# A transformer block pair with product-key experts: 48 instead of 32 tokens by gathered expert rows, the dense part over 208 instead of 224 tokens

## The chip, the cores and the metric

One core of a Trainium2 chip runs the kernel. The metric is the device time of one execution in microseconds; the kernel before has a median of 3184.81 over three runs (3183.85 to 3185.70).

## The reference

256 tokens of width 2048 go through a first block (mixer with a state-space half and an attention half, then an expert layer) and a second one (attention and convolution, cross attention to a memory, a feed-forward part of width 8192). The change is in the expert layer, `peer`: of 16384 experts each token takes 8 x 16, with weights g, by the best sums of two sets of 128 keys.

```
def block(args):
    tb, ib, gb = args
    act = jax.nn.gelu(jnp.einsum('thkd,td->thk', u[ib], tb), approximate=False)
    return jnp.einsum('thk,thkd->td', gb * act, v[ib])
```

u[ib] and v[ib] are rows of two 16384 x 2048 matrices. All is float32.

## The kernel before, in words

**The weight stream.** All weights come as 532 units of 128 x 2048 float32 (1 MB), loaded by SyncE into a ring of four buffers `raw`. Each matmul is done in split precision: ScalarE writes the high part of a unit (`w_hi`, rounded to fp32r; `ahead_first` casts three quarters of it and `ahead_rest` the rest), VectorE writes the low part (`w_lo` = raw - w_hi, line 1033, called `ahead`), and TensorE adds hi x hi, hi x lo and lo x hi. `w_hi` and `w_lo` have two buffers each, so the split of unit u + 2 starts when unit u's matmuls are over, and must be done before unit u + 1's are. The order of the work on each engine is written out by hand, unit by unit; the engines wait for each other by semaphores.

**Dense experts.** Of the 256 tokens the last 224 (`TD`) are computed densely, against all experts, in eight rounds of 2048 experts: 16 u units (`u0` to `u7`: hidden values of 128 experts each) and 16 e units (`e0` to `e7`: 128 output columns each). A matrix of gate values, zero for experts that a token did not pick, is built in u1 (groups of four tokens: one-hot products `pick_a`, `pick_b` on VectorE, lines 1424 and 1429, a matmul, an eviction, blocks of 16 tokens written to DRAM) and read back per round by GpSimd (`load_gates`). In u0 and u1 a unit is 48 single matmuls of 224 columns (`feature_unit`). From e0 on it is a paired unit (`paired_unit`, lines 1768, 1769 and 1774): 16 times one matmul of 448 columns (w_hi against both parts of the activations) and one of 224 (w_lo against the high part).

In rounds 2 to 7 a u unit goes like this: ScalarE copies one half of the sum out of PSUM (line 876), VectorE adds the other (`pair_add`, 1493), ScalarE applies gelu (880), and `gating` on VectorE multiplies by the gates (1447), casts to the high part (1506) and subtracts for the low part (1507). In an e unit `accumulate` adds two halves to `accT` (1486, 1487). At unit 15 of a u half VectorE does the split for the second e unit after the gating, at the others before it.

**Gathered experts.** The first 32 tokens (`G`) are computed from gathered rows. 128 partitions are 4 x 32: partition p holds token p mod 32 and a quarter of its 128 picks. So 32 gathers of 128 rows of u, and 32 of v (GpSimd, line 567, into two buffers `got`), serve all picks. Each gather feeds one *job* on VectorE over 128 x 2048: for u a product with a row sum (1517, with `h_rows`, the normalised tokens), for v a multiply and add into `acc_rows` (1522). The jobs are set between the units by a table: in a round, units 1, 4, 7, 10, 13 of the u half and 0, 2, ... 14 of the e half, 13 jobs. In u7 `sel_rows` adds the four parts with 32 small matmuls (2081), and `sel_add` copies the result to `accT`. In u7 also the memory input is loaded, squared and normalised; in e7 its tiles are turned (`turn_tile`), one per unit.

Of the kernel before, what the change touches and what calls it, by code (L numbers as in the profile page):

```python
# [15 lines left out]
F32 = mybir.dt.float32  # L16
# [21 lines left out]
G = 32  # L38
GROUPS_G, GJ = P // G, PICKS // (P // G)
# [87 lines left out]
def build(nc, x_in, mem_in, stream, cols_in, consts_in, rows_in, wide_in, wdtf_in, keys_in,  # L127
          rel_in, onehot_in, u_rows, v_rows, out):
    ctx = ExitStack()
    with ctx:  # L130
# [47 lines left out]
        row_rs = sb("row_rs", [P, 1])  # L178
# [83 lines left out]
        h_rows = at("h_rows", [P, D], F32, pk)  # L262
        acc_rows = at("acc_rows", [P, D], F32, pk)
# [84 lines left out]
        rows_done = sem("rows_done")  # L348
        s_got = [sem(f"s_got{i}") for i in range(2)]
# [78 lines left out]
        JOBS_U, JOBS_E = (1, 4, 7, 10, 13), tuple(range(0, 16, 2))  # L428
        JOB_AT, _n = {}, 0
        for _r in range(2, PEER_ROUNDS - 1):  # L430
            for _kind, _ks in (("u", JOBS_U), ("e", JOBS_E)):
                for _k in _ks:
                    if _n < 2 * GJ:
                        JOB_AT[_kind, _r, _k] = _n
                        _n += 1
        assert _n == 2 * GJ
        ROW_ACT_AT = next(at for at, n in JOB_AT.items() if n == GJ)
# [68 lines left out]
        def _(pool):  # L506
# [47 lines left out]
            for c in range(GROUPS_G):  # L554
                ps, js = slice(c * G, c * G + G), slice(c * GJ, c * GJ + GJ)
                eng.dma_start(row_idx[ps, :], pick_idx[:, js]).then_inc(s_idx, 16)
                eng.dma_start(row_gate[ps, :], picked[0:G, 0, 2, js]).then_inc(s_idx, 16)
                eng.dma_start(row_rs[ps, :], stat[0:G, 2:3]).then_inc(s_idx, 16)
# [12 lines left out]
            for i in range(2):  # L571
                eng.wait_ge(g_write[i], 16 * (TBLOCKS // 2))
# [6 lines left out]
            eng.wait_ge(s_idx, 16 * 3 * GROUPS_G)  # L579
# [4 lines left out]
            for c in range(GROUPS_G):  # L584
                eng.dma_start(h_rows[c * G:c * G + G, :], x_d[0:G, :]).then_inc(s_rows, 16)
            eng.wait_ge(rows_done, 1)
# [15 lines left out]
            eng.dma_start(wide_l[:, :], wide_in[0:1, :].partition_broadcast(P)).then_inc(s_wide, 16)  # L602
            eng.wait_ge(g_used, 16 * PEER_ROUNDS)
            eng.dma_start(xm[:, :, :], x_d.rearrange("(t p) d -> p t d", p=P)).then_inc(s_xm, 16)
            eng.wait_ge(pow_set, 1)
# [19 lines left out]
        def _(act):  # L625
# [56 lines left out]
            def square(name, src, tt):  # L682

                junk = junk_early if name in ("ln1", "ln2") else junk_cross if name == "gcross" else \
                    acc_rows if name == "gmem" else junk_late
# [183 lines left out]

            for r in range(2, PEER_ROUNDS):  # L870
                for k in range(16):
# [8 lines left out]
                    eng.activation(tmp[:, j, 0:TD], tmp[:, j, 0:TD], ACT.Gelu).then_inc(tmp_full, 1)  # L880
                    if k == 15:
                        ahead_rest(u)
                    if ("u", r, k) == ROW_ACT_AT:
                        eng.wait_ge(got_used, GJ)
                        eng.activation(row_dot[:, :], row_dot[:, :], ACT.Gelu, scale=row_rs[:, :]).then_inc(row_act, 1)
                    if r == PEER_ROUNDS - 1 and k in (6, 8):
                        eng.wait_ge(sel_done, 1)
                        eng.wait_ge(s_mem, 16)
                        square("gmem", mem, (k - 6) // 2)
                if r == PEER_ROUNDS - 1:  # L890
                    break
                for k in range(16):
                    ahead_first(UNIT0[f"e{r}"] + k)
                    ahead_rest(UNIT0[f"e{r}"] + k)
                    if ("e", r, k) == ROW_ACT_AT:
                        eng.wait_ge(got_used, GJ)
                        eng.activation(row_dot[:, :], row_dot[:, :], ACT.Gelu, scale=row_rs[:, :]).then_inc(row_act, 1)
# [8 lines left out]
            for j in range(16):  # L906
                if j == 0:
                    scaled_tile("gmem", 0)
                if j < 15:
                    scaled_tile("gmem", j + 1)  # L910
# [6 lines left out]

# [108 lines left out]
        def _(dve):  # L1026
# [422 lines left out]
            def gated0(g):  # L1449
# [5 lines left out]
                if g % 2 == 0:  # L1455
                    eng.wait_ge(g_write[g // 2], 16 * (TBLOCKS // 2))
# [8 lines left out]
            def gated1(k):  # L1465

                if k == 0:
                    eng.wait_ge(s_idx, 16 * 3 * GROUPS_G)
# [885 lines left out]
```

## Time and profile before

| | before |
|---|---|
| median of 3 runs | 3184.81 us |
| the profiled execution | 3187.75 us |
| its span | 3185.9 us |
| granted TensorE clock, mean | 0.989 |
| TensorE busy | 3067.4 us (96%), 19428 matmuls |
| VectorE busy | 2237.3 us (70%) |
| ScalarE busy | 1400.6 us (44%) |
| data moved | 673 MB, 211 GB/s |

The span runs from the first to the last instruction of the program; the execution's own time is 1.85 us longer. The shares are over the whole span. The dense experts take up the stretch from about 562 to 1946 us: u0, u1, e0 and e1 to 970, then six rounds of a u and an e half. Matmuls overlap each other in the records, so their pace is read from the distance of their starts and not from their durations.

### The profile page before, as it was taken

Reading aid. Unit: us, or ns where it says so; the run is one execution under the profiler, and the core shown is the slowest. Engines: PE = TensorE matmul, PEld = TensorE weight load, DVE = VectorE, ACT = ScalarE, POOL = GpSimd, SP = SyncE. Lnnn points to the kernel's source line nnn. Section 1 sums busy time; section 2 is a strip of 40 time slices with the busy share of each in tenths; the row PEclk is TensorE's granted clock in tenths of the full one; section 3 lists DMA queues with packets and bytes.
Section 4 is the critical chain, followed back from the end, with each engine's and each line's share of the span. In section 5 each row is a group of like instructions: output and inputs, shape, how many; then the busy total and the mean of one; then the engine's idle time right before and its main releaser. Section 6 shows DMA issues by size and latency. Waiting matters only on the chain.

```text
span 3185.9 us, 49641 instructions
## 1 busy us (share of the span) xinstructions
PE 3067.4 (96%) x19428; PEld 2810.2 (88%) x19428; DVE 2237.3 (70%) x3255; ACT 1400.6 (44%) x1640; POOL 143.3 (4%) x168
## 2 busy tenths in 40 slices
PE   6999989999999999999999999999898999999997
PEld 6898879899999999999999999998787888888886
DVE  4666548999867888888888677687655646555564
ACT  3465443356444444444444445334444333333332
POOL 1000000000101101010101000000000000000000
PEclk9999999999999999999999999999999999999999
DMA  4433454456767888888888664544343555555553
GB/s 186 178 141 131 146 197 148 170 189 235 244 245 279 314 300 311 298 310 300 308 298 312 239 238 172 186 166 152 130 174 107 197 190 189 188 188 194 186 188 126
DMA packets 95548, 673.14 MB, mean 211 GB/s; under 512 B 11528, under 2 KB 11552, under 8 KB 15424
## 3 DMA queue, kind: packets, MB, share of 16 engines
q1 hardware_dynamic: 77184, 562.07, 48.9%
q0 software_dynamic: 16224, 94.72, 8.8%
q10 hardware_dynamic: 2016, 14.68, 1.2%
q8 instruction: 80, 1.31, 0.2%
q14 instruction: 44, 0.36, 0.0%
HBM read 652.48 MB, written 18.89 MB: 211 GB/s over the span
## 4 chain that ended last, share of the span: by engine, by line
PE 85%; DVE 11%; ACT 2%; issue 1%; DMA 0%; DVEq 0%; SPq 0%; POOL 0%; POOLq 0%; ACTq 0%
PE bank L1768 29%; PE bank L1769 15%; PE bank L1796 6%; PE bank L1798 6%; PE bank L1797 6%; PE bank L1746 6%; PE bank L1748 5%; PE bank L1747 5%; DVE w_lo L1033 4%; PE bank L1774 2%; DVE pick_a L1429 1%; ACT w_hi L631 1%; DVE pick_b L1424 1%; PE bank L1860 1%; PE bank L1824 1%
## 5 line engine op out<-in xcount | busy, mean ns | idle before, releaser
L1033 DVE TENSOR_TENSOR w_lo<-raw,w_hi 128x2048 fp32r<-128x2048 f32 x532 | 1218.3, 2290 | 570.1 <-ACT w_hi L631 548.1
L1768 PE MATMUL bank<-a_both,w_hi 128*128 128x448 f32 (+1 forms) x3840 | 1258.3, 380 | 6.9 <-DVE a_both L1050 3.9
L1769 PE MATMUL bank<-a_both,w_lo 128*128 128x224 f32 (+1 forms) x4096 | 1060.5, 269 | 0.0
L1768 PEld LDWEIGHTS bank<-a_both,w_hi 128*128 128x128 f32 x3840 | 721.4, 188 | 90.3 <-DVE a_both L1050 4.4
L1769 PEld LDWEIGHTS bank<-a_both,w_lo 128*128 128x128 f32 x4096 | 778.2, 190 | 11.6
L631 ACT ACTIVATE w_hi<-raw 128x2048 fp32r<-128x2048 f32 x308 | 588.4, 1911 | 409.3 <-PE bank L1798 399.7
L1746 PE MATMUL bank<-a_both,w_hi 128*128 128x256 f32 (+1 forms) x1984 | 571.2, 288 | 19.3 <-DVE w_lo L1033 14.0
L644 ACT ACTIVATE w_hi<-raw 128x1536 fp32r<-128x1536 f32 x224 | 333.6, 1489 | 570.2 <-PE bank L1769 568.8
L1747 PE MATMUL bank<-a_both,w_hi 128*128 128x256 f32 (+1 forms) x1984 | 559.2, 282 | 0.0
L1748 PE MATMUL bank<-a_both,w_lo 128*128 128x256 f32 (+1 forms) x1984 | 559.1, 282 | 0.0
L1746 PEld LDWEIGHTS bank<-a_both,w_hi 128*128 128x128 f32 x1984 | 383.4, 193 | 26.9 <-issue 12.5
L1747 PEld LDWEIGHTS bank<-a_both,w_hi 128*128 128x128 f32 x1984 | 383.5, 193 | 0.3
L1748 PEld LDWEIGHTS bank<-a_both,w_lo 128*128 128x128 f32 x1984 | 383.1, 193 | 0.0
L1796 PE MATMUL bank<-w_hi,a_both 128*128 128x512 f32 x960 | 378.6, 394 | 4.3 <-DVE a_both L1677 3.4
L1798 PE MATMUL bank<-w_hi,a_both 128*128 128x512 f32 x960 | 375.8, 392 | 0.0
L1797 PE MATMUL bank<-w_lo,a_both 128*128 128x512 f32 x960 | 375.7, 391 | 0.0
L1796 PEld LDWEIGHTS bank<-w_hi,a_both 128*128 128x128 f32 x960 | 181.8, 189 | 43.1 <-issue 5.0
L1798 PEld LDWEIGHTS bank<-w_hi,a_both 128*128 128x128 f32 x960 | 181.5, 189 | 38.5
L1797 PEld LDWEIGHTS bank<-w_lo,a_both 128*128 128x128 f32 x960 | 181.6, 189 | 37.4
L1768 PE MATMUL bank<-e_both,w_hi 128*128 128x448 f32 x480 | 152.3, 374 | 0.0
L650 ACT ACTIVATE w_hi<-raw 128x512 fp32r<-128x512 f32 x224 | 138.3, 617 | 0.0
L1769 PE MATMUL bank<-e_both,w_lo 128*128 128x224 f32 x512 | 130.3, 265 | 0.0
(314 smaller groups left out, 2436.8 us busy)
## 6 DMA issues: line engine op xcount, KB each, us to landing
raw<-stream_dram SPq DMA_DIRECT2D x532, 1024.0 KB
gates_scratch<-stage ACTq DMA_DIRECT2D x14, 1024.0 KB, 4.8
gbuf<-gates_scratch POOLq DMA_DIRECT2D x30, 448.0 KB, 6.9
x<-x_dram SPq DMA_DIRECT2D x2, 1024.0 KB, 6.5
x_scratch<-x POOLq DMA_DIRECT2D x1, 2048.0 KB, 11.0
wide<-wide_dram POOLq DMA_DIRECT2D x2, 1024.0 KB, 9.0
mem<-mem_dram POOLq DMA_DIRECT2D x1, 2048.0 KB, 9.6
xm<-x_scratch POOLq DMA_DIRECT2D x1, 2048.0 KB, 9.0
```

Source lines behind the costliest of these rows:

```text
L631: eng.activation(w_hi[k % SPLIT][:, :], raw[:, k % RAW, :], ACT.Copy).then_inc(hi_done, 1)
L644: eng.activation(w_hi[k % SPLIT][:, 0:PART], raw[:, k % RAW, 0:PART], ACT.Copy)
L650: eng.activation(w_hi[k % SPLIT][:, PART:UNIT], raw[:, k % RAW, PART:UNIT], ACT.Copy).then_inc(hi_done, 1)
L1033: eng.tensor_tensor(w_lo[k % SPLIT][:, :], raw[:, k % RAW, :], w_hi[k % SPLIT][:, :].bitcast(F32), ALU.subtract).then_inc(split_done, 1)
L1746: mm(o, hi[:, ks], tile(0, kt), start=kt == 0, stop=False)
L1747: mm(o, hi[:, ks], tile(1, kt), start=False, stop=False)
L1748: last = mm(o, lo[:, ks], tile(0, kt), start=False, stop=kt == KT - 1)
L1768: mm(o, hi[:, ks], pair, start=kt == 0, stop=False)
L1769: inst = mm(o2, lo[:, ks], pair[:, 0, :], start=False, stop=False, skip_group_check=True)
L1796: mm(o, tile(0, k0 + k)[:, ts], hi[:, ns], start=first and k == 0, stop=False)
L1797: mm(o, tile(0, k0 + k)[:, ts], lo[:, ns], start=False, stop=False)
L1798: last = mm(o, tile(1, k0 + k)[:, ts], hi[:, ns], start=False, stop=end and k == 3)
```

## The change

- 48 tokens instead of 32 are computed by gathered rows, in two sets: tokens 0 to 31 with four parts of picks, tokens 32 to 47 with eight parts of 16 picks. There are 48 + 48 gathers and jobs instead of 32 + 32, and two tiles `set_rows` in the place of `h_rows` and `acc_rows`.
- The dense part has 208 columns: matmuls of 416 and 208 in the paired units, 208 in u0 and u1, 13 blocks and 52 groups of gate values instead of 14 and 56.
- The table of jobs has 8 in a u half and 10 in an e half, up to u7's unit 11.
- The cast of the activations' high part goes from VectorE to ScalarE, one unit behind: in unit k ScalarE casts that of unit k - 1 after its gelu, and VectorE subtracts for k - 1 after the multiplication by the gates for k. At unit 15 both do 14 and 15.
- `sel_rows` runs once per set (u7 units 3 and 4, e7 units 0 and 1). Squares, normalisation and turns of the memory input move into e7, with two tiles a unit from unit 5 to 9.

```
-G = 32
-GROUPS_G, GJ = P // G, PICKS // (P // G)
+SETS = [(0, 32), (32, 16)]
+G = GJ = sum(n for _, n in SETS)
+SET_DMAS = sum(P // n for _, n in SETS)
...
-        JOBS_U, JOBS_E = (1, 4, 7, 10, 13), tuple(range(0, 16, 2))
+        JOBS = {"u": (1, 3, 5, 7, 9, 11, 13, 14), "e": (0, 2, 3, 5, 6, 8, 9, 11, 13, 15)}
+        JOBS_LAST = (1, 3, 5, 7, 9, 11)
...
+        GMEM_AT = {5 + j: (2 * j, 2 * j + 1) for j in range(5)}
+        GMEM_AT.update({10 + j: (10 + j,) for j in range(6)})
...
-            for c in range(GROUPS_G):
-                eng.dma_start(h_rows[c * G:c * G + G, :], x_d[0:G, :]).then_inc(s_rows, 16)
-            eng.wait_ge(rows_done, 1)
+            for i, (t0, n) in enumerate(SETS):
+                for c in range(P // n):
+                    eng.dma_start(set_rows[i][c * n:c * n + n, :], x_d[t0:t0 + n, :]).then_inc(s_rows, 16)
+            eng.wait_ge(rows_done, len(SETS))
...
+            def cast(r, k):
+
+                eng.wait_ge(g_used, 16 * r + k + 1)
+                eng.activation(a2[0][:, k, 0:TD], tmp[:, k % 4, 0:TD], ACT.Copy).then_inc(act_hi, 1)
...
                     eng.activation(tmp[:, j, 0:TD], tmp[:, j, 0:TD], ACT.Gelu).then_inc(tmp_full, 1)
+                    if k >= 1:
+                        cast(r, k - 1)
                     if k == 15:
                         ahead_rest(u)
+                        cast(r, 15)
...
-                own.do(eng.tensor_copy(a2[0][:, k, 0:TD], t))
-                eng.tensor_tensor(a2[1][:, k, 0:TD], t, a2[0][:, k, 0:TD].bitcast(F32), ALU.subtract).then_inc(tmp_split, 1)
+            def act_lo(r, k):
+
+                eng.wait_ge(act_hi, 16 * (r - 2) + k + 1)
+                eng.tensor_tensor(a2[1][:, k, 0:TD], tmp[:, k % 4, 0:TD], a2[0][:, k, 0:TD].bitcast(F32), ALU.subtract)\
+                    .then_inc(tmp_split, 1)
...
-                    gating(r, k)
+                    gate_hidden(r, k)
+                    if k > 0:
+                        act_lo(r, k - 1)
                     if k == 15:
+                        act_lo(r, 15)
                         ahead(UNIT0[f"u{r}"] + k)
...
-                        eng.tensor_tensor(h_rows[:, :], h_rows[:, :], wide2[:, :], ALU.mult).then_inc(rows_done, 1)
+                        for i in range(len(SETS)):
+                            eng.tensor_tensor(set_rows[i][:, :], set_rows[i][:, :], wide2[:, :], ALU.mult).then_inc(rows_done, 1)
...
-                if k in (2, 3):
-                    sel_rows(k - 2)
+                if k in (3, 4):
+                    sel_rows(0, k - 3)
...
+                if j in (0, 1):
+                    sel_rows(1, j)
+                if j == 5:
+                    eng.wait_ge(sel_added, 2)
                     eng.wait_ge(normed, 6)
```

What stands in a row on the engines at two places (a row is line, operation, output<-inputs, shape; w_lo is the split, `tmp<-tmp,bank` the sum of the halves, `tmp<-tmp,gbuf` the multiplication by the gates, `got,row_dot` or its second row a job).

VectorE, units 14 and 15 of the u half of round 3 and the first e unit, before:

```order
L1493 TENSOR_TENSOR tmp<-tmp,bank 128x224
L1033 TENSOR_TENSOR w_lo_52<-raw,w_hi_50 128x2048
L1447 TENSOR_TENSOR tmp<-tmp,gbuf 128x224
L1506 CAST a_both<-tmp 128x224
L1507 TENSOR_TENSOR a_both<-tmp,a_both 128x224
L1493 TENSOR_TENSOR tmp<-tmp,bank 128x224
L1447 TENSOR_TENSOR tmp<-tmp,gbuf 128x224
L1506 CAST a_both<-tmp 128x224
L1507 TENSOR_TENSOR a_both<-tmp,a_both 128x224
L1033 TENSOR_TENSOR w_lo_53<-raw,w_hi_51 128x2048
L1486 TENSOR_TENSOR accT<-bank,accT 128x224
```

and with the change:

```order
L1517 TENSOR_TENSOR tmp<-tmp,bank 128x208
L1057 TENSOR_TENSOR w_lo_52<-raw,w_hi_50 128x2048
L1471 TENSOR_TENSOR tmp<-tmp,gbuf 128x208
L1532 TENSOR_TENSOR a_both<-tmp,a_both 128x208
L1545 ISA got,row_dot<-got,set_rows_139 128x2048
L1545 ISA row_dot 128x1
L1517 TENSOR_TENSOR tmp<-tmp,bank 128x208
L1471 TENSOR_TENSOR tmp<-tmp,gbuf 128x208
L1532 TENSOR_TENSOR a_both<-tmp,a_both 128x208 x2
L1057 TENSOR_TENSOR w_lo_53<-raw,w_hi_51 128x2048
L1510 TENSOR_TENSOR accT<-bank,accT 128x208
```

The casts are gone, a job stands between units 14 and 15, and the two subtractions for 14 and 15 stand together ahead of the split.

ScalarE at unit 15 of the same half, before:

```order
L644 ACTIVATE w_hi_51<-raw 128x1536
L876 ACTIVATE tmp<-bank 128x224
L880 ACTIVATE tmp<-tmp 128x224
L650 ACTIVATE w_hi_51<-raw 128x512
L644 ACTIVATE w_hi_50<-raw 128x1536
```

and with the change:

```order
L658 ACTIVATE w_hi_51<-raw 128x1536
L900 ACTIVATE tmp<-bank 128x208
L904 ACTIVATE tmp<-tmp 128x208
L892 ACTIVATE a_both<-tmp 128x208
L664 ACTIVATE w_hi_51<-raw 128x512
```

The cast for unit 14 follows the gelu, and the one for unit 15 comes after the rest of the weight cast (a further L892 row).

## Rows read from the trace of the kernel before

**Rows 1.** The page, part 4: the chain that ended last, shares by engine.
```profile
PE 85%; DVE 11%; ACT 2%; issue 1%; DMA 0%; DVEq 0%; SPq 0%; POOL 0%; POOLq 0%; ACTq 0%
```

**Rows 2.** Stretches u3 and e3: length, busy us per engine, PEclk, DMA share, GB/s.
```profile
1133.00:1214.00 81.00, 81.00 (x518) 77.15 (x517) 69.03 (x87) 40.57 (x61) 8.13 (x8) 1.00 0.83 294
1214.00:1293.00 79.00, 79.00 (x505) 75.17 (x504) 64.28 (x69) 32.51 (x34) 8.65 (x9) 1.00 0.86 315
```

**Rows 3.** Timeline of DVE: start, us; splits at the ends of e3 and up1.
```profile
1214.49 2.29 DVE L1033 TENSOR_TENSOR w_lo<-raw,w_hi 128x2048 fp32r<-128x2048 f32 x1
...
1375.27 2.29 DVE L1033 TENSOR_TENSOR w_lo<-raw,w_hi 128x2048 fp32r<-128x2048 f32 x1
...
2634.05 2.29 DVE L1033 TENSOR_TENSOR w_lo<-raw,w_hi 128x2048 fp32r<-128x2048 f32 x1 [3.23 <-ACT w_hi L631]
...
2724.69 2.29 DVE L1033 TENSOR_TENSOR w_lo<-raw,w_hi 128x2048 fp32r<-128x2048 f32 x1
```

**Rows 4.** Timeline of PE: matmuls in u0, the selection in u7, a pair in u4.
```profile
595.87 0.27 PE L1747 MATMUL bank<-a_both,w_hi 128*128 128x224 f32 x1
...
597.54 0.27 PE L1747 MATMUL bank<-a_both,w_hi 128*128 128x224 f32 x1
...
1790.13 1.84 PE L2081 MATMUL bank<-consts,acc_rows 128*128 128x32 f32 x15
...
1340.01 0.26 PE L1769 MATMUL bank<-a_both,w_lo 128*128 128x224 f32 x1
1340.11 0.37 PE L1768 MATMUL bank<-a_both,w_hi 128*128 128x448 f32 x1
```

**Rows 5.** Groups of DVE instructions, whole span: busy, mean ns | idle before.
```profile
L1033 DVE TENSOR_TENSOR w_lo<-raw,w_hi 128x2048 fp32r<-128x2048 f32 x532 | 1218.3, 2290 | 570.1 <-ACT w_hi L631 548.1 <-ACT w_hi L650 8.2
...
L1517 DVE CUSTOM_DVE_ANT_0 got<-got,h_rows 128x2048 f32<-128x2048 f32 x32 | 73.1, 2283 | 0.0
L1522 DVE SCALAR_TENSOR_TENSOR acc_rows<-got,row_gate,acc_rows 128x2048 f32<-128x2048 f32 x31 | 72.7, 2345 | 0.0
...
L1506 DVE CAST a_both<-tmp 128x224 fp32r<-128x224 f32 x96 | 26.6, 277 | 3.3
```

**Rows 6.** Timeline of DVE at the end of u3.
```profile
1213.96 0.38 DVE L1493 TENSOR_TENSOR tmp<-tmp,bank 128x224 f32<-128x224 f32 x1
...
1219.91 2.28 DVE L1033 TENSOR_TENSOR w_lo<-raw,w_hi 128x2048 fp32r<-128x2048 f32 x1
1222.54 0.39 DVE L1486 TENSOR_TENSOR accT<-bank,accT 128x224 f32<-128x224 f32 x1 [0.35 <-PE bank L1774]
```

**Rows 7.** Groups of ACT instructions from 1054 to 1776 us.
```profile
L644 ACT ACTIVATE w_hi<-raw 128x1536 fp32r<-128x1536 f32 x144 | 214.5, 1490 | 373.4 <-PE bank L1769 373.4
L650 ACT ACTIVATE w_hi<-raw 128x512 fp32r<-128x512 f32 x144 | 88.9, 617 | 0.0
L880 ACT ACTIVATE tmp<-tmp 128x224 f32<-128x224 f32 x65 | 25.4, 391 | 20.7 <-DVE tmp L1493 20.7
L876 ACT ACTIVATE tmp<-bank 128x224 f32<-128x224 f32 x65 | 21.9, 337 | 0.0
```

**Rows 8.** PE's waits in u2 and e2: us in total, times, longest.
```profile
PE bank L1768 <- DVE w_lo L1033: 1.8, 1, 1.8
```

**Rows 9.** The chain in u1: two splits with five groups between them.
```profile
746.04 2.20 DVE w_lo L1033
...
756.39 2.20 DVE w_lo L1033
```

**Rows 10.** Stretches after two waits of PE for a split (columns of rows 2).
```profile
1965.00:1968.40 3.40, 3.40 (x16) 3.40 (x17) 3.40 (x3) 0.20 (x1) 0.00 (x0) 0.50 0.70 210
...
994.00:1000.00 6.00, 4.24 (x27) 3.78 (x27) 5.78 (x7) 2.55 (x5) 2.56 (x2) 1.00 0.88 322
```

**Rows 11.** The stretch from 16 to 20 us; gathers: issues, us to landing.
```profile
16.00:20.00 4.00, 0.00 (x0) 0.00 (x0) 2.39 (x2) 2.93 (x3) 0.00 (x0) 1.00 1.01 426
...
got<-u_rows_dram,row_idx POOLq DMA_INDIRECT x32, 5.6
```

More of the change, by code:

```diff
@@ L261, in build @@
         wide2 = at("wide2", [P, D], F32, work_at + 8192)
-        h_rows = at("h_rows", [P, D], F32, pk)
-        acc_rows = at("acc_rows", [P, D], F32, pk)
+        rows_at = work_at + 16384 + 4 * TBLOCKS * 4 * TBLOCK * 4
+        set_rows = [at(f"set_rows{i}", [P, D], F32, rows_at + 8192 * i) for i in range(len(SETS))]
+        assert rows_at + 8192 * len(SETS) <= work_at + WORK
         xm = at("xm", [P, TT, D], F32, work_at + 16384)
@@ L426, in build @@
         PART = 3 * UNIT // 4
-        JOBS_U, JOBS_E = (1, 4, 7, 10, 13), tuple(range(0, 16, 2))
+        JOBS = {"u": (1, 3, 5, 7, 9, 11, 13, 14), "e": (0, 2, 3, 5, 6, 8, 9, 11, 13, 15)}
+        JOBS_LAST = (1, 3, 5, 7, 9, 11)
         JOB_AT, _n = {}, 0
-        for _r in range(2, PEER_ROUNDS - 1):
-            for _kind, _ks in (("u", JOBS_U), ("e", JOBS_E)):
-                for _k in _ks:
+        for _r in range(2, PEER_ROUNDS):
+            for _kind in "ue":
+                for _k in JOBS_LAST if _r == PEER_ROUNDS - 1 else JOBS[_kind]:
                     if _n < 2 * GJ:
@@ L436, in build, with set_of @@
         assert _n == 2 * GJ
+        def set_of(j):
+            return next(i for i, (t0, n) in enumerate(SETS) if t0 <= j < t0 + n)
+        GMEM_AT = {5 + j: (2 * j, 2 * j + 1) for j in range(5)}
+        GMEM_AT.update({10 + j: (10 + j,) for j in range(6)})
         ROW_ACT_AT = next(at for at, n in JOB_AT.items() if n == GJ)
@@ L583, in _ @@
             eng.wait_ge(mm_done, UNIT0["u2"])
-            for c in range(GROUPS_G):
-                eng.dma_start(h_rows[c * G:c * G + G, :], x_d[0:G, :]).then_inc(s_rows, 16)
-            eng.wait_ge(rows_done, 1)
+            for i, (t0, n) in enumerate(SETS):
+                for c in range(P // n):
+                    eng.dma_start(set_rows[i][c * n:c * n + n, :], x_d[t0:t0 + n, :]).then_inc(s_rows, 16)
+            eng.wait_ge(rows_done, len(SETS))
             gather(1)
@@ L906, in _ @@
             for j in range(16):
[L907 to L910, printed above, removed]
+                for kt in GMEM_AT.get(j, ()):
+                    scaled_tile("gmem", kt)
                 if j in (7, 11, 15):
@@ L916, in _ @@
                 ahead_rest(UNIT0["e7"] + j)
+                if j < TT:
+                    eng.wait_ge(sel_done, 1)
+                    eng.wait_ge(s_mem, 16)
+                    square("gmem", mem, j)
             part_square(1, xm, 2)
@@ L1596, in _ @@
             for j in range(16):
-                if j == 0:
-                    scaled_lo("gmem", 0)
-                if j < 15:
-                    scaled_lo("gmem", j + 1)
+                for kt in GMEM_AT.get(j, ()):
+                    scaled_lo("gmem", kt)
                 accumulate(7, j)
                 ahead(UNIT0["e7"] + j)
+                if j == 2:
+                    sel_add(1)
+                    normalise("gmem", mem, mem)
                 if j in (6, 10, 14):
@@ L2075, in _, with sel_rows @@
                 feature("e2", 16, a2_both, r, unit=part_unit, rb=EB, c1=TD, ready=gated_tile("u2", r))
[L2076 removed]
+            def sel_rows(i, h):
+                t0, n = SETS[i]
                 if h == 0:
[L2079 removed]
+                    eng.wait_ge(got_used, GJ + t0 + n)
                 for kt in range(8 * h, 8 * h + 8):
[L2081 removed]
+                    last = mm(bank[(4, 6)[i]][:, kt * n:kt * n + n], set_rows[i][:, kt * P:kt * P + P], C("sel", t0, t0 + n),
+                              start=True, stop=True)
                 if h == 1:
```

86 lines of the change are left out of this document (41 added, 45 removed).

## Prediction

> **What bounds the kernel now.** I read the chain that ended last first: TensorE holds 85% of it and VectorE 11% [rows 1]. Then the table of stretches: in an expert round both halves, the u units (hidden values) and the e units (outputs), show TensorE busy for the whole stretch while VectorE is busy for 69.03 of 81 us and 64.28 of 79 us [rows 2]. So in rounds 2 to 6 the matmuls set the time and VectorE follows with 26.7 us to spare in 160. The starts of the weight split give the pace: 1214.49 and 1375.27 are 32 units apart, 160.78 us or 5.02 us a unit [rows 3]. The question is what a unit costs with 208 columns, and whether VectorE and the transfers still follow.
>
> **Dense units (the gain).** A unit is 16 times a matmul of 448 columns and one of 224, 672 columns in 314 ns. The up units of the last part run 16 times 512 and 256 columns: 90.64 us for 16, 5.66 us a unit, 354 ns for 768 columns [rows 3]. The difference is 40 ns for 96 columns, 0.417 ns a column, which is 2.4 GHz. The change takes away 48 columns, 20 ns, 0.32 us a unit, so 4.70 us. Units of this form: 32 in e0 and e1, 192 in u2 to e7, 224 in all: **-71.7 us**.
>
> The other end: matmuls of 224 columns with a weight load each start 1.67 us apart over 15, 111 ns each, and 15 of only 32 columns take 1.84 us with the last one's own time, some 112 ns apart [rows 4]. There is a floor near 112 ns under a weight load and its matmul. In the paired units the short matmul follows a long one, and its start to the next is 0.10 us [rows 4], already under that floor, and the slope from 768 to 672 columns is whole. I take no floor there. If it held, only the long matmul would gain, 32 columns, 13.3 ns, 0.21 us a unit: -47.7 us. The Trainium skill ("TensorE: Matmul & The Clock Gate", section "LDWEIGHTS (loading the stationary operand)") puts a weight load at its columns over 1.2 GHz, so 107 ns for 128; the 32-column row agrees, the 0.10 us does not. By that page the short matmul could not shrink, and the sum would be the one with -47.7. In u0 and u1 all matmuls are single ones of 224 columns on the floor: I take 0 there (ends 0 and -5).
>
> **VectorE in the rounds.** Of a u unit it loses the cast, 0.28 us, and its operations shrink by 16 columns [rows 5]. Back to back an operation costs a little less than its row says (the sum at 1213.96 is followed after 0.53 us by the split [rows 6], and the long operations overlap their successor by some 0.08: 2.21 for a split of 2.29) a u unit costs 0.53 + 2.21 + 0.30 + 0.31 = 3.35 us, an e unit about 2.92. A job costs 2.21 to 2.35 [rows 5], and a round has 18 instead of 13. Sum per round: 53.6 + 46.7 + 18 x 2.27 = 141.2 us against 32 x 4.70 = 150.4. It follows on the average. In a u unit with a job it needs 5.6 us, without one 3.4; they alternate, and a split two units ahead has a whole unit of room, so the lag of some 1.5 us is made up each time. In the e half two jobs in a row add up to 5.2 twice, then a unit of 2.9: also made up. The exception is the end of the u half.
>
> **The end of each u half.** Before, the last job sits in unit 13 (it delays unit 14's sum to 1213.96, some 1.5 us after that unit's matmuls) and unit 15 comes in time: the split of e1 begins at 1219.91, ends at 1222.20, and unit e0 is over by 1222.54 [rows 6], 0.3 us later. Now a job sits in unit 14, another in 13, and the new order on ScalarE puts the cast of unit 14, the rest of a weight cast and the cast of unit 15 between the last gelu and VectorE's last subtraction, and the split of e1 is queued behind that. Counted from the end of u14's matmuls: the job of 13 ends at 1.5 us, then 0.53 + 2.21 + 0.61 + 2.21 gives 7.06, which is 2.36 after u15's end. Then sum 0.45, gelu 0.40, cast 14 0.30, weight cast 0.60, cast 15 0.34 [rows 7], subtraction 0.35, split 2.29: 7.1 us after u15's end, where e0 ends at 4.7. TensorE waits 2.4 us, in five rounds **+12**. In u7, with its last job in unit 11, the sum starts 0.55 after the matmuls instead of 2.36 and the same count gives 5.3: **+0.6**. Ends: 0 (if the overlaps of short operations are larger than I count) and 3.5 a round.
>
> **The start of u2.** One product over 2048 columns, as long as a split (2.29 us [rows 5]), becomes two ahead of the first job. Before, TensorE waited 1.8 us there [rows 8]. Now 2.2 us more on VectorE, and the unit leaves 0.3 less, while the cast is gone: about 4.4 in all, **+2.5**. The row copies are 12 transfers instead of 4 on GpSimd's queue, issued two and a half units before their use, and a gather on the same queue lands in 5.6 us [rows 11]. I price them at 0 (end +5).
>
> **u1.** With 52 groups of four tokens instead of 56, one of the eleven units with five groups goes. Such a unit takes 10.35 us (746.04 to 756.39) [rows 9], set by VectorE's one-hot products; a unit without groups takes its place, 48 single matmuls at 112 ns [rows 4], 5.4 us: -4.9. The unit with the last groups has two instead of one, but reaches the last later in its matmuls and waits less for it: -2, an estimate. **-7** (ends -3 and -10).
>
> **Last round.** 32 selection matmuls of 16 columns more, at the 112 ns floor [rows 4]: **+3.4**. The squares and the normalisation of mem move from u7 into e7's first three units, where ScalarE and VectorE have half their time free; TensorE asks for them at unit 5. Turn tiles keep their number. Price 0 (ends 0 and +4). If the cover failed, TensorE would wait at e7's unit 5.
>
> **The clock.** After a wait for one weight split TensorE ran 3.4 us at half its clock, 1.2 for 2.4 GHz, 16 matmuls at 0.21 us each; after the wait of 1.8 us at u2's start it kept the full clock [rows 8, 10]. Six of the new waits are longer than that. I take two such drops at 1.7 us: **+3** (ends 0 and +10).
>
> **Transfers.** A round moved 294 GB/s x 81 us + 315 x 79 = 48.7 MB [rows 2]; five more gathers of 1.05 MB make 53.9, in 152.8 us 353 GB/s. The queue has moved 426 GB/s over 4 us at the start [rows 11], and ScalarE's first weight cast has no idle time that a transfer ended [rows 7]. A gather lands in 5.6 us [rows 11] and has two units and more. Price 0.
>
> **Sum:** -71.7 + 12 + 0.6 + 2.5 - 7 + 3.4 + 3 = -57.2. The profiled execution took 3187.75 us, with a span of 3185.9; it would take 3130.6. The median shown is 2.9 below it: 3184.8 - 57.2 = **3128 us**.
>
> **Rivals.**
> 1. *The floor under the short matmul holds in the paired units* (-47.7 for -71.7, and the waits shrink by 1): 3184.8 - 34 = 3151. For it: the single matmuls [rows 4]. Against it: the 0.10 us and the slope. Chance 0.2.
> 2. *The waits at the round ends do not come,* nor the clock drops: 3128 - 16 = 3112. For it: before, the same place fitted by 0.3 us. Against: two jobs in a row ahead of it. Chance 0.1.
> 3. *VectorE sets the pace of rounds 2 to 6.* If two thirds of its 26.7 us of idle time in a round are waits that stay, 141.2 + 17.8 = 159.0 against the 152.8 counted: 5 x 6.2 = +31, 3159. Against: that idle time is waiting for TensorE's unit. Chance 0.1.
> 4. *Transfers become the bound, and it is slower than before.* If the core's queues sustain only what they show over a long stretch, 315 GB/s, a round takes 53.9 / 0.315 = 171 us instead of 160.8: +51 in five rounds, less 64 units x 0.32 = 20.5 in e0, e1, u7 and e7, less 7, plus 3.4: +27, 3212. It decides from the point where under 335 GB/s are sustained (53.9 MB in 160.8 us). For it: a busy share of 0.86 at 315. Against: 426 at the start, and no wait on a transfer. Chance 0.06.
> 5. *The gain goes in small waits of all kinds,* nothing to measure: chance 0.02.
>
> **How the numbers follow.** The forecast has 0.52, with its own range 3116 to 3140. From 3108 to 3156 it takes in rivals 1 and 2; rivals 3 to 5, 0.18, lie outside. A measurement of this kernel tells 0.2% (6 us) from no change. Faster: 0.52 + 0.2 + 0.1 + 0.1, 0.92; within 0.2%: 0.02; slower: 0.06.
>
> **What would show it.** Splits 32 units apart in a round at 150.4 plus 2.4 us; TensorE's idle time on the weight split some 2.4 us at the second unit of each e half and 4.4 at u2's fifth unit, and nowhere else in the rounds; u1 7 us shorter; starts of paired matmuls 294 ns apart by pairs (301 for rival 1). Idle time of the jobs on a gather, or of ScalarE's weight cast on the stream, would prove rival 4; idle time before many splits, rival 3. A VectorE without waits for TensorE at the u half would make the forecast wrong.

## The result and the profile after

The changed kernel takes 3165.43 us (median of four, 3165.13 to 3166.53) beside 3184.62 for the kernel before: a ratio of 0.994, interval 0.9923 to 0.9957. That is 19.2 us less, where 57 were forecast, and outside the range of 3108 to 3156. The profiled execution took 3166.53 us with a span of 3164.7.

The chain that ended last (page, part 4) answers to [rows 1]:

```profile
PE 81%; DVE 13%; ACT 2%; issue 2%; DMA 1%; POOL 0%; DVEq 0%; SPq 0%; POOLq 0%; ACTq 0%
```

TensorE gave up four points of it, and a transfer has one per cent where it had nothing. To see where, I cut both traces at the starts of the weight splits (a stage is from the split two units ahead of its first unit to the next such split), all in us:

| stage | before | after | difference | forecast by the sum |
|---|---|---|---|---|
| u0 | 96.84 | 97.82 | +1.0 | 0 |
| u1 | 151.90 | 145.59 | -6.3 | -7 |
| e0, e1 | 159.57 | 153.20 | -6.4 | -10.3 |
| u2 | 83.61 | 94.54 | +10.9 | -2.6 |
| e2 to e6 | 722.30 | 705.42 | -16.9 | -31.1 |
| u7 | 84.19 | 80.92 | -3.3 | -4.5 |
| e7 | 86.20 | 87.60 | +1.4 | -1.7 |
| u0 to e7 | 1384.61 | 1365.08 | -19.5 | -57.2 |

(The row of e2 to e6 has the u halves between them; its forecast is 144 units x 0.32, 12 for the waits and 3 for the clock.) Two rows are wrong by more than 10 us, u2 and the long middle one, and e0 and e1 are wrong in the same way as the middle.

**The pace.** The same two splits as in [rows 3], 32 units apart, by the timeline of VectorE (start, us; in brackets the idle time before and what ended it):

```profile
1207.24 2.29 DVE L1057 TENSOR_TENSOR w_lo<-raw,w_hi 128x2048 fp32r<-128x2048 f32 x1 [0.50 <-DVE tmp L1517]
...
1363.51 2.29 DVE L1057 TENSOR_TENSOR w_lo<-raw,w_hi 128x2048 fp32r<-128x2048 f32 x1
```

156.27 us for 160.78. A wait of 1.71 us lies between them, so the units took 154.56, 0.19 us less each where 0.32 was forecast. The pairs of matmuls in the same round (timeline of PE):

```profile
1330.09 0.37 PE L1800 MATMUL bank<-a_both,w_hi 128*128 128x416 f32 x1
1330.30 0.26 PE L1801 MATMUL bank<-a_both,w_lo 128*128 128x208 f32 x1
1330.40 0.37 PE L1800 MATMUL bank<-a_both,w_hi 128*128 128x416 f32 x1
```

A long matmul starts 0.31 us after the one before it, not 0.294; over e0 and e1 it is 0.299 (153.20 us for 512 pairs).

**Waits.** TensorE's waits from 955 to 1041 us (u2), and from 1041 to 1753 (us in total, times, longest); in the kernel before, the first was 1.8 [rows 8] and the second did not exist:

```profile
PE bank L1800 <- DVE w_lo L1057: 13.7, 1, 13.7
...
PE bank L1800 <- DVE w_lo L1057: 8.4, 5, 1.7
```

The five are at the second unit of e2 to e6, where the prediction had put five of 2.4. The 13.7 us are new in kind. What stood before them is in the chain from 955 to 1000 us (start, us, what):

```profile
960.37 5.32 POOL set_rows L598 x11
965.69 17.73 DMA set_rows<-x_scratch
983.48 2.17 issue
```

and VectorE's timeline shows who waited:

```profile
973.34 0.37 DVE L1532 TENSOR_TENSOR a_both<-tmp,a_both 128x208 fp32r<-128x208 f32 x1
983.45 4.49 DVE L1615 TENSOR_TENSOR set_rows<-set_rows,wide 128x2048 f32<-128x2048 f32 x2 [9.74 <-DMA set_rows<-x_scratch]
987.97 2.29 DVE L1545 CUSTOM_DVE_ANT_0 got<-got,set_rows 128x2048 f32<-128x2048 f32 x1
...
990.70 2.29 DVE L1057 TENSOR_TENSOR w_lo<-raw,w_hi 128x2048 fp32r<-128x2048 f32 x1
```

VectorE stood still for 9.74 us behind the twelve row copies that the prediction had priced at 0, and the split for TensorE's next unit was queued behind the two products and the job. While the copies ran, the transfers were busy nearly all the time and moved half of what they had moved at such a share elsewhere (stretches; columns of [rows 2]):

```profile
964.00:968.00 4.00, 4.00 (x28) 3.95 (x28) 2.37 (x2) 2.27 (x4) 2.18 (x5) 1.00 1.08 219
968.00:972.00 4.00, 4.00 (x28) 3.95 (x27) 2.11 (x4) 2.80 (x5) 0.00 (x0) 1.00 0.94 188
972.00:976.00 4.00, 4.00 (x29) 3.95 (x28) 1.70 (x3) 2.24 (x3) 0.00 (x0) 1.00 1.07 221
...
984.00:988.00 4.00, 0.00 (x0) 0.00 (x0) 3.96 (x3) 0.00 (x0) 0.00 (x0) 0.54 0.21 86
...
992.00:998.00 6.00, 4.87 (x17) 4.74 (x18) 5.85 (x8) 2.00 (x5) 2.96 (x2) 0.50 0.97 375
```

A busy share of 1 gave 426 GB/s in [rows 11] and gives 188 to 221 here. From 964 to 968 us it was the row copies' queue alone (set 0's copies had landed by 968.7); after that set 1's eight copies shared the transfers with the weight stream and moved 0.82 MB in 12 us, 68 GB/s. The last two rows show the clock: it was at half from 984.3 to 998.0 us, so it fell during the wait and stayed there for 4.9 us of work after it, which began at 993.13.

**Transfers in the rounds** (stretches u3 and e3):

```profile
1129.00:1207.00 78.00, 78.00 (x517) 76.98 (x516) 67.57 (x76) 43.89 (x75) 10.94 (x12) 1.00 0.94 340
1207.00:1285.00 78.00, 76.27 (x506) 75.31 (x506) 69.78 (x71) 33.47 (x38) 10.31 (x11) 1.00 0.94 352
```

340 and 352 GB/s for 294 and 315 [rows 2]: the queues carried the five more gathers, and TensorE's only wait in them is the one for the split.

### The profile page after: what moved, and what is told of

Same layout as the page of the kernel before. It is cut to its first block, busy times and chain, and to the rows that moved or that the text cites. A ratio compares the mean times of both kernels' runs of the same rounds, so it can differ in the third digit from the quotient of the medians.

```text
span 3164.7 us, 49740 instructions
## 1 busy us (share of the span) xinstructions
PE 3026.0 (96%) x19428; PEld 2810.9 (89%) x19428; DVE 2259.4 (71%) x3189; ACT 1418.2 (45%) x1732; POOL 189.0 (6%) x232
## 4 chain that ended last, share of the span: by engine, by line
PE 81%; DVE 13%; ACT 2%; issue 2%; DMA 1%; POOL 0%; DVEq 0%; SPq 0%; POOLq 0%; ACTq 0%
PE bank L1800 26%; PE bank L1801 13%; PE bank L1828 6%; PE bank L1829 6%; PE bank L1830 6%; PE bank L1778 6%; PE bank L1780 6%; PE bank L1779 6%; DVE w_lo L1057 4%; PE bank L1806 2%; DVE pick_a L1453 1%; ACT w_hi L645 1%; DVE pick_b L1448 1%; PE bank L1892 1%; DMA set_rows<-x_scratch 1%
## 5 line engine op out<-in xcount | busy, mean ns | idle before, releaser
L1800 PE MATMUL bank<-a_both,w_hi 128*128 128x416 f32 (+1 forms) x3840 | 1226.8, 377 | 27.4 <-DVE w_lo L1057 23.5
L1801 PE MATMUL bank<-a_both,w_lo 128*128 128x208 f32 (+1 forms) x4096 | 1041.6, 264 | 0.0
L1800 PE MATMUL bank<-e_both,w_hi 128*128 128x416 f32 x480 | 146.0, 367 | 0.0
L1801 PE MATMUL bank<-e_both,w_lo 128*128 128x208 f32 x512 | 127.1, 258 | 0.0
```

Source lines behind the costliest of these rows:

```text
L1800: mm(o, hi[:, ks], pair, start=kt == 0, stop=False)
L1801: inst = mm(o2, lo[:, ks], pair[:, 0, :], start=False, stop=False, skip_group_check=True)
```

## The experiments

Theory at this point: (A) the short matmul of a pair is on a floor, so only the long one became cheaper; (B, my forecast) every column counts, and something else eats the gain. For u2 the rivals are: the copies are slow by their source, their number, their bytes or their destination. For the round ends they are the job in unit 14, or the new order of operations.

### The short matmul, 208 for 224 columns, in the kernel before

```
+                    m = 208 if n == TD else n
-                    inst = mm(o2, lo[:, ks], pair[:, 0, :], ...)
+                    inst = mm(o2[:, 0:m], lo[:, ks], pair[:, 0, 0:m], ...)
```

> The kernel before, with the short matmul of the 224 paired units over 208 of its 224 columns; the long one keeps 448. Left out: the product of the weights' low part with 16 tokens' activations. Theory A (weight load and short matmul share a floor that 224 columns already lie under): 0 us, the stretch e0 stays at 79.2 us and starts of paired matmuls stay at 312 ns by pairs. Theory B (my forecast: every column counts, 0.417 ns): 6.7 ns a pair, 0.107 us a unit, -24 us, e0 at 77.5 us.

Measured: 3185.61 us, ratio 1.000 (0.999 to 1.001). The splits of [rows 3] in this run:

```profile
1213.28 2.29 DVE L1033 TENSOR_TENSOR w_lo<-raw,w_hi 128x2048 fp32r<-128x2048 f32 x1
...
1374.11 2.29 DVE L1033 TENSOR_TENSOR w_lo<-raw,w_hi 128x2048 fp32r<-128x2048 f32 x1
```

160.83 us for 160.78. Sixteen columns less in each of 3584 matmuls changed nothing, so theory B is ruled out for this matmul.

### The long matmul, 2 x 208 for 2 x 224 columns, in the kernel before

```
+                        m = 208 if n == TD else n
-                        mm(o, hi[:, ks], pair, ...)
+                        mm(o[:, :, 0:m], hi[:, ks], pair[:, :, 0:m], ...)
```

> The kernel before, with the long matmul of the 224 paired units over 2 x 208 of its 2 x 224 columns; the short one keeps 224. Left out: the product of the weights' high part with 16 tokens' activations. Theory A (only the short matmul is on a floor) and theory B both give 13.3 ns a pair, 0.213 us a unit, -47.7 us, e0 at 75.9 us. A third theory (the changed kernel's loss of gain comes from somewhere else, such as the data path of the activations) gives less than that. Together with the run of the short matmul it says which of the two matmuls gave what the change gained a unit, 0.20 us.

Measured: 3143.61 us, ratio 0.9871 (0.9854 to 0.9887), -41 us.

```profile
1198.25 2.29 DVE L1033 TENSOR_TENSOR w_lo<-raw,w_hi 128x2048 fp32r<-128x2048 f32 x1
...
1353.21 2.29 DVE L1033 TENSOR_TENSOR w_lo<-raw,w_hi 128x2048 fp32r<-128x2048 f32 x1
```

154.96 us, 5.82 less for 32 units: 0.182 us each. The changed kernel's 0.19 is all here. The time is a little above what both theories gave (0.213 a unit).

### The short matmul at 64 columns, in the kernel before

```
+                    m = 64 if n == TD else n
```

> The kernel before, with the short matmul of the 224 paired units over only 64 of its 224 columns. Left out: the product of the weights' low part with 160 tokens' activations. Dropping 16 columns there had changed nothing, and dropping 64 of 256 in the up parts gained 2.0 of 90.6 us. Theory A (the floor is that of the weight load, whatever the matmul): 0 us again, e0 at 79.2 us. Theory A2 (the floor is lower and 208 columns only just reached it, something else paces these units): 160 columns at 0.417 ns would be up to 67 ns a pair, so a gain of tens of us.

Measured: 3189.29 us, ratio 1.0017 (1.0005 to 1.0029).

```profile
1214.01 2.29 DVE L1033 TENSOR_TENSOR w_lo<-raw,w_hi 128x2048 fp32r<-128x2048 f32 x1
...
1375.44 2.29 DVE L1033 TENSOR_TENSOR w_lo<-raw,w_hi 128x2048 fp32r<-128x2048 f32 x1
```

161.43 us: 160 columns less in the short matmul save nothing and even cost 0.02 us a unit. Its pairs (timeline of PE):

```profile
1340.15 0.44 PE L1768 MATMUL bank<-a_both,w_hi 128*128 128x448 f32 x1
1340.43 0.19 PE L1770 MATMUL bank<-a_both,w_lo 128*128 128x64 f32 x1
1340.46 0.45 PE L1768 MATMUL bank<-a_both,w_hi 128*128 128x448 f32 x1
```

From the short start to the next long start there are now 0.03 us, and 0.28 from the long to the short one; the pair takes 0.31 as before. So the distance of starts inside a pair says nothing of a floor: the floor moves between the two, and only the pair's sum can be read.

### The short matmul of the up units, 192 for 256 columns, in the kernel before

```
+                    m = 192 if n == T else n
```

> The kernel before, with the short matmul of the 64 paired units of the up parts over 192 of its 256 columns (the long one keeps 512). Left out: the product of the weights' low part with 64 tokens' activations there. Theory A (floor of 112 ns under a weight load and its matmul; single matmuls of 256 columns start 120 ns apart): only the first 8 ns of 27 are gained, an up unit goes from 5.66 to 5.53 us, -8.5 us in all. Theory B (every column counts, 0.417 ns): 27 ns a pair, 5.24 us a unit, -27 us. Theory C (the floor lies lower, at the 101 ns seen from a short to the next long start): 16 to 19 ns, 5.38 us, -18 us.

Measured: 3179.29 us, ratio 0.9977 (0.9967 to 0.9986). The start and end of up1, as in [rows 3]:

```profile
2628.89 2.29 DVE L1033 TENSOR_TENSOR w_lo<-raw,w_hi 128x2048 fp32r<-128x2048 f32 x1 [3.23 <-ACT w_hi L631]
...
2717.50 2.29 DVE L1033 TENSOR_TENSOR w_lo<-raw,w_hi 128x2048 fp32r<-128x2048 f32 x1
```

88.61 us for 90.64: 7.9 ns a pair where 64 columns at full worth are 27. Theory A had said 8. So at 256 columns the short matmul is still 8 ns above the floor, at 224 it is on it. This is where my slope went wrong: it was taken from 768 to 672 columns, across the edge, and used below it. The edge is only a part of it. The pair of 512 and 192 columns takes 346 ns (88.61 us for 256) and the pair of 448 and 224 takes 314, both with the short matmul on the floor, so the long one's 64 columns are worth 32 ns where 2.4 GHz gives 27. The slope looked whole because the long matmul gave more than its columns while the short one gave less. Why the long one did, in another part of the program, no run shows.

### Row copies from different rows, in the changed kernel

```
-  eng.dma_start(set_rows[i][c * n:c * n + n, :], x_d[t0:t0 + n, :])
+  eng.dma_start(set_rows[i][c * n:c * n + n, :], x_d[c * n:c * n + n, :])
```

> The changed kernel, with the row copies of u2 taking different rows of the scratch array for each of their 12 parts (rows 0 to 127 for either set) in place of the same 32 and 16 rows four and eight times. As many transfers and bytes. So the gathered experts' hidden values are computed from the wrong tokens. TensorE's wait at u2's fifth unit is 13.7 us now. Theory D1 (reading the same rows of DRAM again and again halves the rate, packets of 8 KB take 0.6 us instead of 0.31): the packets take 0.31 us, 2 MB land in 5 to 6 us and the wait falls to about 4 us, -10 us. Theory D2 (the number of transfers, 12 on GpSimd's queue, some of 16 rows) or D3 (2 MB beside the weight stream are too much for the transfers whatever they read): it stays at 13.7 us, 0.

Measured: 3165.18 us, ratio 0.9936 (0.9919 to 0.9953). TensorE's wait in u2:

```profile
PE bank L1800 <- DVE w_lo L1057: 12.8, 1, 12.8
```

Of 13.7 us 12.8 are left. The source is not the cause. The transfers from 968 to 976 us still moved 203 and 217 GB/s.

### Row copies spread over the partitions, in the changed kernel

```
-                    ps, js = slice(c * n, c * n + n), slice(c * n, c * n + n)
+                    ps, js = slice(c, P, P // n), slice(c * n, c * n + n)
-  eng.dma_start(set_rows[i][c * n:c * n + n, :], x_d[t0:t0 + n, :])
+  eng.dma_start(set_rows[i][c:P:P // n, :], x_d[t0:t0 + n, :])
-        *[(p % n == np.arange(n)[None, :]) ...
+        *[(p // (P // n) == np.arange(n)[None, :]) ...
```

> The changed kernel with the parts of the picks laid out the other way: partition p holds token p div 4 (p div 8 in set 1), so each of the 12 row copies writes every fourth or eighth partition instead of 32 or 16 neighbours. Same transfers, bytes and source rows. The run with different source rows had left TensorE's wait in u2 at 12.8 us (13.7 before it), so the source is not the cause. Theory D4 (writing into few neighbouring partitions is slow: packets of 0.6 us, 220 GB/s for 32 partitions and less for 16): packets take near 0.31 us, the 2 MB land some 6 to 7 us after the first issue, the wait falls to about 4 us, -9 us. Theory D2 (the number of transfers on GpSimd's queue) or D3 (2 MB beside the stream): the wait stays at 13 us, 0.

Measured: 3158.48 us, ratio 0.9913 (0.9896 to 0.9929), 7 us below the changed kernel (9.3 from u0 to e7). Stretches while the copies ran, set 0's first:

```profile
963.00:966.00 3.00, 3.00 (x22) 2.96 (x21) 0.74 (x2) 2.02 (x3) 3.00 (x7) 1.00 1.04 407
966.00:970.00 4.00, 4.00 (x28) 3.94 (x27) 2.67 (x3) 1.69 (x3) 0.53 (x2) 1.00 1.04 297
970.00:974.00 4.00, 4.00 (x29) 3.94 (x28) 3.23 (x4) 1.95 (x6) 0.00 (x0) 1.00 1.02 244
```

and the waits of TensorE and of VectorE from 955 to 1020 us:

```profile
PE bank L1800 <- DVE w_lo L1057: 5.2, 1, 5.2
...
DVE set_rows L1615 <- DMA set_rows<-x_scratch: 1.3, 1, 1.3
```

The same bytes by the same number of transfers, with other destinations: set 0's four went at 407 GB/s instead of 219, VectorE waits 1.3 us for them instead of 9.7, and TensorE 5.2 instead of 13.7. The destination is the cause of those 8.5 us. Of the other 5.2, 1.3 are the last of the transfers and the rest is VectorE's own queue. The Trainium skill ("SBUF — State Buffer", section "Door 1: The DMA port swizzle") says that the rate of a transfer follows from how many of 16 ports its partitions reach, each with a sixteenth of 435 GB/s: 32 neighbouring partitions reach 8, so 218 GB/s; the measured 219 of set 0's copies agrees. By its formula every fourth partition reaches all 16 (407 measured, 396 of it by the row copies' queue), and every eighth only 8. That last part is not tested here: from 970 to 974 us the row copies' queue moved 0.57 MB, 143 GB/s, beside 0.39 MB of the weight stream, still more than the 68 GB/s of set 1's copies in the changed kernel.

### Set 1's copies and product late, in the changed kernel

```
-        wide2 = at("wide2", [P, D], F32, work_at + 8192)
+        wide2 = at("wide2", [P, D], F32, a2_at + 16384)
...
+            copy_rows(0)
+            gather(1)
+            copy_rows(1)
...
-                    if (r, k) == (2, 1):
+                    if (r, k) in ((2, 1), (2, 5)):
```

> The changed kernel, with set 1's eight row copies issued behind the second gather and its product with the weights' row at u2's unit 5 instead of 1, and that row kept in another place (so that the gathers need not wait for it). Set 0's four copies and product stay at unit 1. The 13.7 us that TensorE waits in u2 now should fall: theory F1 (set 1's transfers were what was late; VectorE stood still behind them): the first wait becomes that of the kernel before or less, 1 to 2 us, and the second product fits: -11 to -13 us and 2 more with the clock, which ran at half for 13.7 us behind that wait. Theory F2 (the slow transfers hold up the weight stream or the gathers wherever they stand): a wait of 5 us or more comes back at units 5 to 8, -5 us.

Measured: 3150.68 us, ratio 0.9887 (0.9871 to 0.9904), 14.8 us below the changed kernel. TensorE's waits from 955 to 1020 us:

```profile
PE bank L1804 <- DVE w_lo L1061: 3.3, 2, 1.6
```

One of 1.6 us is at the fifth unit, as in the kernel before, and one of 1.6 comes behind the second product, which shares its unit with a job. The stretch from u0 to e7 is 12.6 us shorter (1352.44). Theory F1 was right in its size: the eight slow copies still ran, but nobody waited for them. F2's second wait came too, behind the product and not behind a transfer (VectorE shows no wait for one there).

### Unit 15 in the order of the others, in the changed kernel

```
-                    if k < 15:
-                        ahead(UNIT0[f"u{r}"] + k)
+                    ahead(UNIT0[f"u{r}"] + k)
                     gate_hidden(r, k)
...
-                    if k < 15:
-                        ahead_rest(u)
+                    ahead_rest(u)
                     eng.wait_ge(pair_sum, 16 * (r - 2) + k + 1)
```

> The changed kernel, with unit 15 of each u half ordered like the others: VectorE does the split for the second e unit right after the sum, ahead of the gates and the two subtractions, and ScalarE the rest of the weight cast ahead of the gelu. TensorE waits 1.65 to 1.71 us for that split now in five rounds, and lost its clock once behind one. Theory E1 (the split is late because it stands behind the last unit's chain): those waits go, -8.4 us, less 1.7 with the drop of the clock; the last subtraction then comes some 4.0 us into e0, which needs it at 4.4. Theory E2 (the wait moves: e0's sixteenth pair waits for the activations instead): the time changes by less than 2 us, and TensorE shows waits for a_both in every round.

Measured: 3158.62 us, ratio 0.9925 (0.9907 to 0.9943). TensorE's waits from 1041 to 1753 us:

```profile
PE bank L1796 <- DVE a_both L1530: 6.5, 5, 1.6
```

The five waits for the split became five for the activations, as E2 says, 1.9 us less in all: the rounds of u3 and e3 and of u4 and e4 are 0.3 us shorter each (156.33 for 156.62, 156.02 for 156.32). The median came down by more, 6.8 us. From u0 to e7 the profiled executions differ by 3.0 (1362.06 for 1365.08), and 1.6 of that is a clock drop in e5 that did not come; the rest of the 6.8 lies outside this stretch, in parts that the edit doesn't touch. At a round's end VectorE was late by itself, whatever the order.

### Jobs out of unit 14, on top of set 1 late

```
-        JOBS = {"u": (1, 3, 5, 7, 9, 11, 13, 14), "e": (0, 2, 3, 5, 6, 8, 9, 11, 13, 15)}
-        JOBS_LAST = (1, 3, 5, 7, 9, 11)
+        JOBS = {"u": (1, 3, 5, 7, 9, 11, 13), "e": (0, 2, 3, 5, 6, 8, 9, 11, 12, 14, 15)}
+        JOBS_FIRST = (3, 7, 9, 11, 13)
+        JOBS_LAST = (1, 3, 5, 6, 8, 10, 11, 13)
```

> As the run with set 1 late, and the jobs set otherwise: u halves 1, 3, 5, 7, 9, 11, 13 (u2: 3, 7, 9, 11, 13), e halves 0, 2, 3, 5, 6, 8, 9, 11, 12, 14, 15, u7: 1, 3, 5, 6, 8, 10, 11, 13. No job stands in unit 14 of a u half, nor two in a row ahead of unit 15. Theory G1 (the wait of 1.7 us at each round end comes from the job in unit 14): the five waits go, -8 us and a drop of the clock, on top of the former run: about 3143 us. Theory G2 (VectorE has too little room for a seventh job per u half and an eleventh per e half): waits on splits appear inside the e halves and the gain is half of that or less.

Measured: 3139.47 us, ratio 0.9854 (0.9837 to 0.987): the fastest here, 26 us below the changed kernel. The kernel before had a median of 3186.50 beside this run, so it is 47 below that one. TensorE's waits from 1041 to 1730 us, and the two splits of [rows 3]:

```profile
PE bank L1805 <- DVE w_lo L1062: 1.7, 5, 0.3
```

```profile
1189.49 2.29 DVE L1062 TENSOR_TENSOR w_lo<-raw,w_hi 128x2048 fp32r<-128x2048 f32 x1
...
1344.44 2.29 DVE L1062 TENSOR_TENSOR w_lo<-raw,w_hi 128x2048 fp32r<-128x2048 f32 x1
```

The five waits are 0.3 us each now, the round takes 154.95 us, and no wait appears inside an e half with eleven jobs: G1, not G2.

### The same with the spread layout

```
-                    ps, js = slice(c * n, c * n + n), slice(c * n, c * n + n)
+                    ps, js = slice(c, P, P // n), slice(c * n, c * n + n)
...
```

> The changed kernel with set 1's copies late, the jobs set otherwise (3139 us as measured) and the parts of the picks laid out across the partitions (the spread layout, -7 us by itself, its wait in u2 5.2 us). Theory J1 (both cures act on the same wait, which is already gone): 3139 us, 0 to -1 against that run. Theory J2 (the copies slowed the weight stream too, or the wider spread also serves other waits): up to 3 us more.

Measured: 3142.97 us, ratio 0.9866 (0.985 to 0.9883), 3.5 us above the run before it. Cut at the splits, u0 to e7 take 1341.40 us against 1341.08: u2 is 0.75 us shorter (78.40 for 79.15), u0 1.0 longer, and the rest of the difference lies outside, in ck, out2 and up0. So J1: nothing more to win where nobody waits. That u0 is 96.8 or 97.8 us long, in either kernel, goes with the clock. In the seven of the fourteen profiled executions with 97.8 (the changed kernel's is one) the granted clock was at half for 3.4 us from 591 to 594 us on, and in none of the seven with 96.8. (A drop between 576 and 584 us costs nothing that shows: 96.84 us with it in the kernel before, 96.84 without any in the run with 192 columns.) The stretch in the changed kernel's trace:

```profile
591.80:595.20 3.40, 3.40 (x19) 3.40 (x17) 3.37 (x12) 0.00 (x0) 0.00 (x0) 0.50 0.73 296
```

### The cast back on VectorE, in the changed kernel

```
-                    if k >= 1:
-                        cast(r, k - 1)
...
-                eng.wait_ge(act_hi, 16 * (r - 2) + k + 1)
+                own.do(eng.tensor_copy(a2[0][:, k, 0:TD], tmp[:, k % 4, 0:TD]))
...
-                    if k > 0:
-                        act_lo(r, k - 1)
+                    act_lo(r, k)
```

> The changed kernel with one part undone: the activations' high part is cast by VectorE, in the same unit as the gates, as in the kernel before; jobs, columns and row copies stay as changed. Theory H1 (with 8 jobs in a u half VectorE has no room for 16 casts of 0.28 us, 4.5 us a half): new waits of TensorE on splits inside the u halves and a longer one at their ends, +1 to +3 us a round, +5 to +15 us. Theory H2 (the room is there; the cast on ScalarE only lengthens the chain at unit 15, where three more operations of ScalarE stand): the wait of 1.7 us at the round ends stays or gets shorter, the time within 3 us of the changed kernel's 3165.

Measured: 3165.16 us, ratio 0.9936 (0.9919 to 0.9953): the changed kernel's time. TensorE's waits from 1060 to 1758 us:

```profile
PE bank L1796 <- DVE w_lo L1054: 8.6, 5, 1.7
```

8.6 us for 8.4: as H2 says, the room is there. The rounds are longer by 0.2 to 0.9 us (156.78 for 156.62, 157.19 for 156.32), u7 by 0.6, and no clock drop came behind a round end.

### Only the cast on ScalarE, in the kernel before

The diff is the cast's part of the change by itself.

> The kernel before, with only the cast moved to ScalarE, one unit behind, with VectorE's subtraction one unit behind too; 32 tokens, 224 columns and the old table of jobs. My forecast priced the order of ScalarE at unit 15 (cast 14, rest of the weight cast, cast 15) at 1.2 us ahead of the last subtraction. Theory I1 (that order matters by itself): the split of the second e unit ends some 0.7 us later than e0, five waits of 0.3 to 0.7 us, +2 to +4 us. Theory I2 (without a job in unit 14 VectorE is early enough): 0, within 1 us of the kernel before.

Measured: 3184.91 us, ratio 1.0001 (0.9991 to 1.0011). TensorE's waits from 1060 to 1750 us:

```profile
PE bank L1783 <- DVE w_lo L1042: 0.8, 5, 0.2
```

The waits of I1 are there, five of 0.2 us at the round ends; a round takes 161.12 us for 160.78. Against that u2's wait is 1.3 instead of 1.8 us. The median doesn't show either. So the move of the cast gains nothing with 13 jobs a round. With 18 it does: in the run with the cast back on VectorE the stretch from e2 to u7 is 3.1 us longer, clock drop aside. Its profiled execution has neither that drop (1.6) nor the half clock in u0 (1.0), and such differences between executions are as large as the effect, so the median doesn't show it.

## Why the prediction was wrong, step by step

- **Dense units, -71.7: this step failed.** The pace fell by 0.19 us a unit in the rounds and 0.20 in e0 and e1, some -42.6 in all. It was rival 1's mechanism: only the long matmul's 32 columns count, and the runs with 208, 64 and 192 columns show the floor directly. The evidence that I set against it was misread twice. "Its start to the next is 0.10 us, already under that floor" took one part of a pair for its pace; with 64 columns that part is 0.03 us, and the pair takes the same. "The slope from 768 to 672 columns is whole" was the slope across the edge: 8 of its 40 ns are the short matmul's, and 32 the long one's for 64 columns, more than the 27 they are worth at 2.4 GHz. Read as sums, the old rows would have told it: 312 ns less the 112 of a floor leave 200 for 448 columns, of which 187 are the columns at 2.4 GHz. With the same 13 on top 416 columns need 187, and the pair 299, which is what e0's starts give. The rule of the Trainium skill on weight loads ("TensorE: Matmul & The Clock Gate", section "LDWEIGHTS (loading the stationary operand)"), which I had named and gone against, was the better guide; its 107 ns are some 5 below the 112 that a weight load with a short matmul takes here. Rival 1's -47.7 is still 5 too much: 0.19 a unit in the rounds for its 0.213. The rest is missing in the u halves: between the starts of their last matmuls the units of e3 take 4.80 us, 0.22 less than before and the full worth, and those of u4 take 4.85, 0.17 less (medians of 15 distances, 5.02 before in both). Why the u halves give less stays open.
- **The start of u2, +2.5: this step failed too.** It was +14.3: 11.9 us of wait more, and 2.4 for 4.9 us of work at half clock. The terms of VectorE were right (with the spread copies the wait is 5.2, of which 1.3 is the last of the transfers; 4.4 was counted); the failure is "I price them at 0 (end +5)" for the row copies. I compared them with a gather, which writes all 128 partitions, and looked at the four of before as harmless because nobody had waited for them, though the same stretch before already moved only 269 GB/s at a busy share of 1.06 (976 to 981 us). The second half of the error is the product of both sets in one place: set 1 isn't needed before its first job, the 33rd, in e3.
- **The round ends, +12:** place, number and mechanism were right, the size 8.4. The chain was counted with durations from the rows, and operations that follow each other overlap (ScalarE's cast starts 0.29 us after the gelu, which itself lasts 0.38). The split came 6.4 us after unit 15's end, for 7.1. That it is the job in unit 14 is shown by the run without it; u7, without such a job, had no wait (forecast +0.6). The new order of ScalarE at unit 15 alone is a wait of 0.2 a round.
- **u1, -7:** -6.3. **The last round, +3.4:** u7 and e7 lost 1.9 together where the columns alone gave some -6, so +4. The 32 selection matmuls at 112 ns are 3.6 (the forecast has 3.4 for them), and 0.8 is a wait in e7 for VectorE's part of a tile of the memory input, the end of my range there.
- **The clock, +3:** of the five round-end waits one was followed by a drop (1.7 us); the one in u2 is counted above, and the half clock at 591.8 us in u0 cost 1.0. **VectorE and the transfers:** both followed, as forecast; rivals 3 and 4 did not come. VectorE even had room for the casts that were taken from it, at a price of some 3 us.
- **Sum, on the stretch u0 to e7:** -42.6 + 14.3 + 8.4 - 6.3 + 4.2 + 1.7, and 1.0 for the clock in u0: -19.3; measured -19.5.

**The range** took in rival 1 at 3151, but beside it no second error. 3151 and the +12 from the copies give 3163.

## What to carry to other kernels

Read a matmul's price from the distance between repeats of the whole pattern, at two sizes on the same side of the floor and in the same part of the program; the distance between unlike neighbours is not a price. Before a copy is doubled, look at what it moves per busy share and at how many partitions it writes, and ask who is queued behind it on its reader. A table of fillers should leave free the last two units before a place where one engine's chain ends in another's start.

## What the runs showed of the hardware

- A weight load with a matmul started every 112 ns whether the matmul had 224 or 208 columns (u0 of the two kernels) or 32 or 16 (the selections of the changed one). As the short one of a pair with 448 columns it cost the same with 224, 208 or 64 columns (312 to 315 ns a pair), and beside 512 columns 8 ns more at 256 than at 192.
- Copies of 8 KB rows into 32 neighbouring partitions moved 219 GB/s at a busy share of 1.08; into every fourth partition, with a little of the weight stream, 407 GB/s at 1.04.
- Waits of 1.65 to 1.71 us of TensorE were followed by a drop of the clock in none to two of five cases, and not always the same one (none of five with VectorE's casts, one in the changed kernel, two with the copies from different rows). Parts that no edit touched differ by 1 to 3 us between executions with the drops in them (ck and cv together 52.25 or 53.74, out2 107.0 to 110.3), so for effects below that the stages and not the medians decide.
